# One layer pair with 32 experts on one core: products on parts of TensorE's array, VectorE sums in place of products, later loads, and another end

## The reference

```
block 1: h = rmsnorm(x); z = h @ w_in                      # 1024 x 8840 columns
  swa : sliding window attention, 8 heads of 64, bias by distance, sinks
  conv: gated depthwise convolution, 31 taps, layernorm, silu
  fox : 8 heads of 64; logits + c_q - c_k, c = cumsum(log_sigmoid(f)); causal softmax
  moba: 8 heads of 64 (one block of 256, so plain causal), bias by distance
  x += (sum over 4 branches of sigmoid(gate) * (branch @ w_br)) @ w_out
  x += (silu(g) * v) @ w_down, (g, v) = conv of 3 taps of rmsnorm(x) @ w_up
  x = rmsnorm(x) * final_g
block 2: pooled windows and differential attention (4 heads, 2 score maps each,
         mask by chunks of 64 tokens), @ w_out_2, added to x
  cross attention, 4 heads of 256, with a memory of 256 tokens
  experts: logits = h @ w_router; the best 4 of 32; softmax over them;
         y = sum of gate * expert(h), expert: 1024 -> 2048 (clamped swiglu) -> 1024
  return rmsnorm(x + y) * final_norm_g_2
```

## Time and profile before

| | |
|---|---|
| time, median of 3 runs | 1753.46 us (1751.78 to 1754.3) |
| the profiled execution: time, span | 1753.44 us, 1751.6 us |
| mean granted TensorE clock | 0.987 of full speed |
| TensorE, VectorE, ScalarE, GpSimd busy | 92%, 43%, 28%, 10% |
| moved by DMA | 526.44 MB, mean 301 GB/s |
| the stages by the trace, us | start to 141, attention to 305, mixing and feed-forward to 576, block 2 to 782, router to 802, experts to 1738 |

### The profile page before, as it was taken

One profiled execution on the slowest core, in us unless ns is written; L12 is line 12 of the kernel. 1 busy time (PEld: TensorE's weight loads), 2 busy tenths in 40 slices (PEclk: granted clock), 3 DMA queues, 4 the chain that ended last, 5 costly groups with the idle time before them and its releaser, 6 DMA issues.

```text
span 1751.6 us, 22754 instructions
## 1 busy us (share of the span) xinstructions
PE 1607.4 (92%) x9732; PEld 1015.8 (58%) x9732; DVE 751.4 (43%) x1330; ACT 483.4 (28%) x822; POOL 166.6 (10%) x199
## 2 busy tenths in 40 slices
PE   6999999999999999989999898988888888888885
PEld 6899889989999989984333232323232322323221
DVE  6798765788894678643122121212121212111112
ACT  4445655446554536532011010101010101010001
POOL 1200001503540040110000000000000000000000
PEclk9999999999999999998999999999999999999998
DMA  8754334546655534656999999999999999999994
GB/s 200 204 178 156 117 112 146 167 145 184 183 188 189 179 121 152 221 219 262 405 426 426 426 427 426 425 426 425 426 427 426 426 427 426 426 426 427 427 426 196
DMA packets 194553, 526.44 MB, mean 301 GB/s; under 512 B 18745, under 2 KB 136542, under 8 KB 145294
## 3 DMA queue, kind: packets, MB, share of 16 engines
q1 hardware_dynamic: 190720, 519.34, 76.3%
q0 software_dynamic: 3184, 5.37, 1.6%
q10 hardware_dynamic: 542, 0.21, 0.0%
HBM read 523.24 MB, written 1.61 MB: 300 GB/s over the span
## 4 chain that ended last, share of the span: by engine, by line
PE 43%; DMA 42%; DVE 9%; ACT 3%; issue 1%; SPq 1%; ACTq 1%; DVEq 0%
PE bank L600 42%; DMA slot_ring<-in_w_down 16%; DMA slot_memx<-in_w_down 10%; DMA slot_late<-in_w_down 8%; DMA slot_high<-in_w_down 8%; DVE slot_ring_r L1896 2%; ACT high_r L1479 1%; DVE conv L1904 1%; SPq L1262 1%; ACTq L1535 1%; ACT dscore L1479 0%; DVE rstd L1938 0%; DVE rot_tmp L2330 0%; DMA slot_ring<-in_w_in 0%; DVE x_sb L1904 0%
## 5 line engine op out<-in xcount | busy, mean ns | idle before, releaser
L1896 DVE TENSOR_TENSOR slot_ring_r<-slot_ring,high_r 128x1024 fp32r<-128x1024 f32 x198 | 247.1, 1290 | 96.7 <-ACT high_r L1479 94.2
L600 PE MATMUL bank<-h_hi_r,high_r 128*128 128x256 f32 x1000 | 286.4, 286 | 1.5 <-DVE slot_ring_r L1896 1.3
L600 PE MATMUL bank<-h_lo_r,high_r 128*128 128x256 f32 x1000 | 283.5, 284 | 0.0
L1900 DVE TENSOR_SCALAR ga<-bank 128x512 f32<-128x512 f32 x32 | 22.1, 692 | 579.6 <-PE bank L600 579.6
L600 PE MATMUL bank<-h_hi_r,slot_ring_r 128*128 128x256 f32 x952 | 269.9, 283 | 0.0
L1479 ACT ACTIVATE high_r<-slot_ring 128x1024 fp32r<-128x1024 f32 x198 | 198.0, 1052 | 61.6 <-PE bank L600 42.0
L600 PEld LDWEIGHTS bank<-h_hi_r,high_r 128*128 128x128 f32 x1000 | 191.5, 192 | 4.3 <-DVE slot_ring_r L1896 2.4
L600 PEld LDWEIGHTS bank<-h_lo_r,high_r 128*128 128x128 f32 x1000 | 191.8, 192 | 0.1
L1479 ACT ACTIVATE th_e<-ga 128x512 f32<-128x512 f32 x32 | 20.2, 630 | 612.4 <-DVE ga L1900 612.4
L600 PEld LDWEIGHTS bank<-h_hi_r,slot_ring_r 128*128 128x128 f32 x952 | 182.5, 192 | 0.0
L600 PE MATMUL bank<-slot_ring,xg 128*64 128x512 f32 x528 | 124.6, 604 | 11.7 <-DMA slot_ring<-in_w_gu 11.7
(11 more groups left out here) (433 smaller groups left out, 2912.1 us busy)
## 6 DMA issues: line engine op xcount, KB each, us to landing
slot_ring<-in_w_gu SPq DMA_DIRECT2D x66, 1024.0 KB, 26.3
slot_high<-in_w_gu SPq DMA_DIRECT2D x50, 1024.0 KB, 26.7
slot_ring<-in_w_down SPq DMA_DIRECT2D x49, 1024.0 KB, 26.5
slot_last<-in_w_gu SPq DMA_DIRECT2D x38, 1024.0 KB, 26.7
slot_ring<-in_w_in SPq DMA_DIRECT2D x36, 1024.0 KB, 5.0
slot_late<-in_w_gu SPq DMA_DIRECT2D x32, 1024.0 KB, 26.4
slot_high<-in_w_down SPq DMA_DIRECT2D x25, 1024.0 KB, 26.9
slot_ring<-in_w_up SPq DMA_DIRECT2D x44, 512.0 KB, 4.5
```

The costliest lines, as they stand in the source:

```text
L600: return e.matmul(o, lhs, rhs, start=start, stop=stop, skip_group_check=True)
L1896: return e.tensor_tensor(o, i, j, op)
L1900: return e.tensor_scalar(o, i, s1, None, op1)
```

## The change

- Attention: `scores` and `values` go through the three kinds in one order, in which neighbouring products use different halves of the array (64 rows, or 64 columns); moba takes its heads in pairs the other way round for that (`half_of`).
- fox: the two-row products go. Two transposes of the forget rows give c_q as columns, a DRAM copy (`fox_dram`) is read back by GpSimd as a row for all partitions (`fox_row`), masked there, and VectorE adds both in the pass that added the mask.
- `dscores`: no `chunk1` products; the two maps of a head alternate by array half. VectorE writes NEG over the masked corner and takes the next head's maxima before this head's difference.
- `final_g` is applied to x in the out2 stage, two tiles before each residual.
- Router: product k goes to column group k modulo 4; one product with `stack` adds the four and turns them.
- Start: parameter rows in four parts around ScalarE's first work; constants are loaded ahead of qa 0; the bias products stand after qa 1, the rows `more cols` inside ub 0; the root of `gain_sq` is taken before `block2`.
- End: in experts 2 to 5 a product with the identity adds x_tok to the banks; the flag is read at expert 2; the last expert's hidden rows are turned in another bank before `scatter(30)`; the last norm reads the banks and stores four pieces.

```diff
+    parts["stack"] = (i[:, None] % NE == np.arange(NE))
...
-    parts["chunk1"] = np.where(k // CHUNK <= q // CHUNK, 0.0, NEG)
...
+            return n // 2 + 4 * (n % 2) if kind == SWA else n ^ 1 if kind == MOBA else n
+
+        def half_of(kind, n):
+            i = (n + (kind == MOBA)) % 2
+            return slice(i * HD, (i + 1) * HD)
...
-            turn_rows("more cols", (1, 2, 3))
 
             for c in range(BT):
-                project(("ub", c), hs, h_of("ln1_g"), (dve, ("glu", c)))
-                if c == 0:
...
+                project(("ub", c), hs, h_of("ln1_g"), (dve, ("glu", c)),
+                        between=None if c else lambda: turn_rows("more cols", (1, 2, 3)))
...
+            q.wait_ge(*dve["forget rows"])
+            for t in range(TT):
+                m = e.transpose(bank("forget columns")[:, t * FOX_H:(t + 1) * FOX_H], zz[:, t * P:(t + 1) * P], ident[0:FOX_H, 0:FOX_H])
...
+            def scores(n):
+
+                for kind in KINDS:
+                    banks.take(q, ("scores", kind, n))
...
+                for kind, i in ((SWA, 0), (MOBA, 0), (FOX, 0), (MOBA, 1), (SWA, 1), (FOX, 1)):
+                    pair, r = n // 2, half_of(kind, n)
+                    qt, kt = {SWA: (qa[r, pair, :], ka[r, :]), MOBA: (qd[r, pair, :], kd[r, pair, :]),
+                              FOX: (qc[r, pair, :], kc[r, pair, :])}[kind]
+                    b, c = bank(("scores", kind, n)), PARTS[i]
+                    qs, ks = ((slice(128, 256), slice(0, 256)), (slice(0, 128), slice(0, 128)))[i]
+                    m = matmul(b[:, c], qt[:, qs], kt[:, ks], True, True)
+                    if i:
+                        m.then_inc(*pe.step("scores", kind, n))
+                        banks.give(("scores", kind, n), (dve, ("biased", kind, n)))
...
+                for kind, kb in ((SWA, 0), (MOBA, 0), (FOX, 0), (MOBA, 1), (SWA, 1), (FOX, 1)):
+                    r = half_of(kind, n)
+                    o = bank(("heads", kind, pair))[r, 0:S]
+                    v = {SWA: va[:, kb, r], MOBA: vd[:, kb, pair * P + r.start:pair * P + r.stop],
+                         FOX: vc[:, kb, pair * P + r.start:pair * P + r.stop]}[kind]
+                    q.wait_ge(*act["probs", kind, n])
+                    if kb:
+                        matmul(o[:, 128:256], v, prob[kind][:, 256:384], False, True).then_inc(*pe.step("values", kind, n))
+                    else:
+                        matmul(o, v, prob[kind][:, 0:256], True, False)
...
+                for c, qs, ks in ((PARTS[0], slice(128, 256), slice(0, 256)), (PARTS[1], slice(0, 128), slice(0, 128))):
+                    for m in range(2):
+                        name, r = ("dscores", head, m), slice(m * HD, (m + 1) * HD)
+                        last = matmul(bank(name)[:, c], uq[r, head, qs], uk[r, head, ks], True, True)
...
-                m = matmul(b[0:NE, 0:S], wrt[:, k, :], h[:, k, :], k == 0, k == KT - 1)
+                m = matmul(b[k % 4 * NE:(k % 4 + 1) * NE, 0:S], wrt[:, k, :], h[:, k, :], k < 4, k >= 4)
...
-                            m = e.transpose(b[:, S + s * NE:S + (s + 1) * NE], mean_sb[0:NE, s * P:(s + 1) * P], ident[0:NE, 0:NE])
+                            m = matmul(b[:, S + s * NE:S + (s + 1) * NE], mean_sb[:, s * P:(s + 1) * P], C("stack"), True, True)
...
+            def add_x(r):
+
+                t, c = r // 2, r % 2
+                q.wait_ge(*act["x_tok", t, c])
+                matmul(y_acc[r][:, :], ident, x_tok[:, t, c * 512:(c + 1) * 512], False, False).then_inc(*pe.step("x added", r))
...
+                if n == NE - 1:
+                    q.wait_ge(*dve["slot gate", n])
+                elif n:
+                    down_free(q, n)
...
-                    m = e.transpose(b_down[:, j * P:(j + 1) * P], pair[:, :, j % 2], ident)
+                    m = e.transpose(turned(n)[:, j * P:(j + 1) * P], pair[:, :, j % 2], ident)
...
-                q.wait_ge(*acts["y hi", n])
-                q.wait_ge(*dves["y lo", n])
-                for part in (y_hi, y_lo):
+                for part, done in ((y_hi, acts["y hi", n]), (y_lo, dves["y lo", n])):
+                    q.wait_ge(*done)
...
+                if n == 2:
+                    q.wait_ge(*dve["flag"])
+                    above = e.value_load(flag_sb[0:1, 0:1], min_val=0, max_val=S)
...
-                if n >= 2:
+                if 2 <= n < NE:
...
+                    if n == NE and k == 5:
+                        scatter(q, n - 2)
+                    if 2 <= n < 6 and k == 3:
+                        add_x(n - 2)
...
-                if name == ("ub", 1):
+                if name == ("qa", 0):
...
+            for r in range(4):
+                t, cs = r // 2, slice(r % 2 * 512, (r % 2 + 1) * 512)
+                q.wait_ge(*dve["out", r])
+                e.dma_start(outv[:, t, cs], y_sb[:, t, cs]).then_inc(*out_stored.step("out", r))
+            q.wait_ge(*out_stored["out", 3])
...
+            e.dma_start(fox_dram, ez).then_inc(*fox_out.step("fox"))
+
+            def fox_rows(n):
+
+                row = fox_row[n % 2]
+                if n >= 2:
+                    q.wait_ge(*dve["biased", FOX, n - 2])
+                q.wait_ge(*fox_out["fox"])
+                for c, w in ((0, S), (S, P)):
+                    e.dma_start(row[:, c:c + w], fox_dram[n:n + 1, 0:w].broadcast_to([P, w])).then_inc(*fox_ins[n % 2].step("fox", n))
+                q.wait_ge(*fox_ins[n % 2]["fox", n])
+                if n:
+                    q.wait_ge(*pool["fox", n - 1])
+                masked = row[:, P:3 * P].rearrange("p (c k) -> p c k", c=2)
+                e.tensor_tensor(masked, masked, C("causal")[:, P:2 * P].rearrange("p (c k) -> p c k", c=1).broadcast_to([P, 2, P]),
+                                ALU.add).then_inc(*pool.step("fox", n))
...
+                if n == 7:
+                    fox_rows(0)
+                    fox_rows(1)
+                elif n >= 9 and n % 2:
+                    fox_rows(n // 2 - 2)
...
+            load_rows(0)
             q.wait_ge(*first_in["first"])
             sqrt_table()
+            load_rows(3)
+            load_rows(2)
...
+            load_rows(1)
...
+            sqrt_table()
+            q.wait_ge(*dve["gain squares"])
+            af(gain_sq, gain_sq, ACT.Sqrt).then_inc(*act.step("gain root"))
             act.mark("block2")
             after_all(q, "block2")
-            sqrt_table()
             for i in range(4):
...
+                if n == NE - 1:
+                    sqrt_table()
...
+            for r in (0, 1, 2):
+                af(y_sb[:, r // 2, r % 2 * 512:(r % 2 + 1) * 512], bank(("y", r))[:, :], ACT.Square, scale=D ** -0.5,
+                   accum_out=scal[:, 8 + r:9 + r]).then_inc(*act.step("out squares", r))
+            q.wait_ge(*dve["out sums"])
+            af(scal[:, 12:14], scal[:, 12:14], ACT.Sqrt, bias=eps_col[EPS2]).then_inc(*act.step("out root"))
...
+                if kind == "fox":
+                    q.wait_ge(*dve["forget columns"])
+                    q.wait_ge(*pool["fox", n])
...
+                    if kind == "fox":
+                        stt(sc[:, c], b[:, c], forget_cols[:, t * FOX_H + n:t * FOX_H + n + 1], fox_row[n % 2][:, c], ALU.add,
+                            ALU.add).then_inc(*dve.step("biased", kind, n))
+                    else:
+                        tt(sc[:, c], b[:, c], toep[i % 8][:, cs], ALU.add).then_inc(*dve.step("biased", kind, n))
...
+                    if norm == "xattn_g":
+                        q.wait_ge(*act["square", "final_g", 3])
+                        apply("final_g", x, x, steps=(2 * i, 2 * i + 1))
+                        own()
...
-            q.wait_ge(*act["square", "final_g", 3])
-            apply("final_g", x, x)
...
+                    unseen = b[0:CHUNK, P:3 * P].rearrange("p (c k) -> p c k", c=2)[:, :, CHUNK:P]
+                    e.memset(unseen, NEG).then_inc(*dve.step())
...
+            dmaxima(0)
+            for head in range(DIFF_H):
+                if head + 1 < DIFF_H:
+                    dmaxima(head + 1)
+                difference(head)
...
+            last = x_tok[:, 1, 512:D]
+            e.tensor_copy(last, bank(("y", 3))[:, :]).then_inc(*dve.step())
+            own()
+            e.scalar_tensor_tensor(out=y_sb[:, 1, 512:D], in0=last, scalar=1.0 / D, in1=last, op0=ALU.mult, op1=ALU.mult,
+                                   accum_out=scal[:, 11:12]).then_inc(*dve.step())
+            q.wait_ge(*act["out squares", 2])
+            own()
+            e.tensor_reduce(scal[:, 12:14], scal[:, 8:12].rearrange("p (t c) -> p t c", t=TT), AX.X, ALU.add).then_inc(*dve.step("out sums"))
+            q.wait_ge(*act["out root"])
             q.wait_ge(*fg_in["fg"])
-            for t in range(TT):
-                r = scal[:, 8 + t:9 + t]
-                q.wait_ge(*act["out root", t])
-                e.reciprocal(r, r).then_inc(*dve.step())
-                own()
```

(7 more changed lines are left out.)

233 lines of the change are left out of this document (98 added, 135 removed).

## The result

The changed kernel takes 1738.75 us (median of 5 runs, 1735.63 to 1742.37), the kernel before 1754.08 in the same comparison: a ratio of 0.992, 95% interval 0.9909 to 0.9932, or 15.3 us faster. The forecast was 1717.4 with a range from 1706 to 1732: the sign was right, the size less than half of it, and the time lies outside the range. The profiled execution took 1737.07 us with a span of 1735.3, so its span is 16.3 us shorter than that of before, where 36.0 were forecast.

The account below looks back on a forecast made before the run. It took TensorE to bound the stages before about 802 us and DMA the expert stream after; gains of 4.9, 15.5, 1.4, 9.8, 3.0 and 6.5 less 5.1 made 36.0, so 1753.4 became 1717.4 us, range 1706 to 1732.

Parts of the forecast that it names:

- The stream: Expert weights: DMA-bound at 29.4 us an expert, shifting as a whole, one to one with TensorE's start on expert 0.
- a rival in which the stream doesn't move: Expert weights: bound by DMA from earlier on, so only the end gives, 6.5 us: 1747 us; chance 0.05.
- signs of being wrong: Attention turns above 19.5 us, TensorE waiting for GpSimd's rows there, or the stream's start moving by less than 20.
- Start: Before attention: earlier first table load and no TensorE waits for split units, 4.9 us gained, between 2 and 7.
- Attention: Eight turns: array halves overlap and fox's two-row products go, 15.5 us gained, bounds 8 and 20.
- Rival 1: Attention: VectorE bounds every turn, so attention gives 8 us: 1725 us; chance 0.2.
- Score maps: Score maps: VectorE begins sooner and a head costs it less, 9.8 us gained, bounds 7 and 12.
- final_g: Norm moved into the out2 stage: its VectorE work costs 5.1 us there, bounds 3.5 and 6.
- Router: Router: four column groups keep up with VectorE's tiles, 3.0 us gained, bounds 0 and 3.5.
- table: Opening of block2: no table load there any more, 1.4 us gained with the spare activation behind it.
- end: After the last weights: earlier down(31), scatter, shorter last norm and smaller store, 6.5 us gained, bounds 4.5 and 10.
- rival 5: Attention: GpSimd's fox rows come late and the score pass waits; 10 us late gives 1777 us; chance 0.03.

Follow-up runs that it names:

- the changed kernel again: The changed kernel profiled once more with nothing changed: 1737.67 us, 0.9922 of the kernel before.
- few_taps: The changed kernel without the last 5 of the convolution's 31 taps: 1732.96 us.
- slots_back: The changed kernel with its first eight weight slots at the SBUF addresses of the kernel before: 1729.25 us, 0.9859 of the kernel before.
- one_half: The changed kernel with all three kinds of a head set on the same half of TensorE's array: 1743.41 us.
- final_first: slots_back with the norm of block 1 (final_g) applied by VectorE ahead of the score maps again: 1725.1 us.
- final_on_pool: slots_back with the norm of block 1 scaled by GpSimd, its reciprocal on VectorE behind the score maps: 1723.9 us, 0.9838 of the kernel before.
- before_again: The kernel before profiled once more with nothing changed: 1753.56 us.
- late_flag: The changed kernel with the overflow flag read at the end again, ahead of each engine's branch: 1737.36 us.

## Why the prediction was wrong, point by point

**The stream: the step that failed.** The prediction took 29.4 us an expert from the rate of before and let the stream shift "as a whole". It has a rival in which the stream doesn't move, and none in which it is slower. Measured: the start moved by 19.9 us and the landing of the last weights by 7.6, so a term that the sum had at nothing was 12.3: 10.4 of a slower stream and 2.0 of a low clock ahead of its first product. The cause of the slower stream is shown by moving slots alone, in both kernels and both ways: -8.4 us in the changed kernel, +10.5 in the one before. The diff has the line; I read it as bookkeeping. Why it takes a row of units off the multiple for packets to get longer isn't settled. It fits that the packets of the changed kernel stay at 309 ns until 832 us, while the stream still has gaps, and get longer when it has none. Two of the prediction's own signs of being wrong came true: the stream's start moved by less than 20 us, and two turns of attention stayed above 19.5 (25.9 and 20.5). The Trainium skill, DMA: Bandwidth & Descriptors, section How a descriptor splits into AXI transactions, says for reads that each transaction starts at a multiple of 256 bytes, so that a descriptor off it needs one more and moves bytes for nothing. By it an 8 KB row at 128 past would be 260 beats of 32 bytes instead of 256, 1.6%, an estimate of 14 us for the stream; the runs show the same boundary for writes into SBUF, 1.3% and 10 us, and, against it, next to no loss (309.8 ns for 309.4) with one group of slots on the multiple.

**Start: right in sum.** 5.0 for 4.9. The first unit began at 17.63 us instead of 20.32, though ScalarE's first table load came at 3.85 and not near 9.3. Behind the first unit, the 3.9 us of waits for split units shrank to 0.7 in this profile; the changed kernel again has 1.5, few_taps 2.9 and slots_back none, so this term is worth 1 to 3.9 us, and 5.0 is in part luck.

**Attention: the size of the first half was wrong.** (The turns of the prediction add up to 15.4, not 15.5.) For turns 4 to 7 the forecast of 11.4 came out at 11.5, though not as composed: scores and values gave 2.5 a turn, not 2.9, each turn has 0.2 to 0.3 us of waiting for fox's softmax, and turns 5 and 7 of the kernel before had a lower clock (0.91, 19.5 us a turn instead of 18.0), which is gone. Without these the gain would be 8.5: two errors cancel, and the match is luck. For turns 0 to 3 it said +4.0 and they lost 2.2: turn 1 lost 4.4 and turn 3 1.0, and turns 0 and 2 gained 3.2. Rival 1 was true there: VectorE's order puts the taps ahead of the scores, few_taps shows it (6.1 us back), and one_half shows that the halves are worth nothing in these turns. What I left out is the second step: waits of TensorE in a row, 0.3, 1.3, 0.6 and 1.3 us, and then its clock at the lower level for a unit (2.6 us more). Turn 3 has waits of 1.1, 1.3 and 0.6 us and a clock of 0.79 behind them. The rule of the Trainium skill behind rival 1 (TensorEngine Tiling (Array Packing), PSUM Bottleneck) holds for half of the turns.

**Score maps: right.** 10.2 for 9.8; VectorE from the first memset to the last difference 16.7 us, as forecast. But final_first shows what was whose. The stage takes 42.7 us in the kernel before, 38.0 in final_first and 34.2 in slots_back: 4.7 come from the other edits and 3.9 from final_g being moved. The changed kernel's profile has 32.6, 1.6 less; its clock in that stretch is 1.00, that of slots_back 0.95.

**final_g: too small.** 7.8 for 5.1. VectorE's 5 us are there: TensorE waits 4.2 us for GpSimd's squares behind them and 1.1 for ScalarE's, where it waited 0.9 before. The rest is the next unit at a clock of 0.71, which final_on_pool gets back. The move as such was a loss: 3.9 gained, 8.1 paid.

**Router, table, end: near.** Expert 0 gained 2.6 for 3.0, the table 0.8 for 1.4. The end gained 8.8 for 6.5 in this pair of profiles; 2.9 of that is the low clock of down(31) in the profile of before, from which the sum was read, and against before_again it is 5.8. The issue time at the branch stayed, 1.33 for 1.67, as the rule of the Trainium skill had it (Runtime: NRT & Kernel Launch, Instruction fetch mechanics); no run took the fetch away, so that it is the cause isn't shown. But late_flag has 2.31, so a read of the flag that has long been done does help by 1.0. GpSimd's fox rows (rival 5) were never late: no wait of VectorE for them.

## What to carry to other kernels

Where a stage is bound by DMA, look at every edit that moves the destination tiles, and keep the start of each at a multiple of 256 bytes of SBUF, with the base of the allocation counted in: it is worth 8 to 11 us here, as much as the whole of attention (9.3). Before moving work from one stage to another, ask in which of the two the engine is the bound, and price the move at both ends: 3.9 us for 8.1. When TensorE gets faster, count the waits that replace its work as longer than they are, since a unit after several short waits ran near half clock here. And compare the same event in both traces, and look at more than one profile of each kernel: the landing of another unit of weights would have made the stretch from expert 0 to the last landing 9.8 us longer and not 12.3, and a stretch at low clock in one profile made the end's gain 8.8 and not 5.8.

## What the runs showed of the hardware

The address of a DMA's destination sets its rate at the limit of the engines: 313.9 ns an 8 KB packet with no slot on a multiple of 256 bytes (fourteen of fifteen at 128 past it), 309.8 or 309.9 with seven on it, 309.4 with fourteen on it, in nine, ten and one profiles. Products on different halves of the array overlap for plain fp32: the six products of a head set's scores take 1.50 us, against 2.16 where all are on one half (one_half). And GpSimd scaled eight tiles of 128x256 in 14.4 us (0.9 to 1.1 and 0.7 to 1.0 us a pass). VectorE's reciprocals beside it stayed at 1.74 us, but its passes with two tensors as inputs got longer: 0.63 to 0.95 us instead of 0.48 for three of four scalings, 0.96 instead of 0.43 for a subtraction. With VectorE's added reciprocal this is the wait of 2.4 us that TensorE has for `mix_lo` in final_on_pool and not in slots_back.
